# Seven block products for all but two gate/up pairs of each FFN, with their weight sums made in DRAM

## The chip, the cores and the metric

The kernel runs on one core of a Trainium2 chip. The metric is the device time of one launch in microseconds (us); the runs shown are three launches, and one more launch was taken by the profiler.

## The reference

One step of a two-layer decoder over 544 token columns (512 of a new sequence, 8 groups of 4 running ones). Each layer is FFN 1, a mixer with three recurrent branches, and FFN 2. An FFN of width 2816 on a model width of 1024 is

```
h = rmsnorm(x, g)
gate, up = split(h @ w_up, 2)          # w_up is 1024 x 5632
x = x + 0.5 * ((silu(gate) * up) @ w_down)
```

All in float32.

## The kernel before

**Tiling.** Activations lie transposed: 128 rows of a feature tile by 544 token columns. A weight tile ("piece") is 128 x 1024, that is eight 128 x 128 blocks along the contraction. Every product is done in three matmul passes on split operands: a high part (rounded to the matmul's format) and a low part (the rest) of weights and of activations, as high x high, high x low and low x high. A dense tile is 8 blocks x 3 passes x 2 halves of 272 columns, 48 matmuls (`dense`, L536).

**Two gate/up tiles as one 2 x 2 problem.** A gate tile and its up tile together are a 2 x 2 block matrix (gate or up, first or second half of the contraction) times activations in 2 x 2 blocks (halves of contraction and of tokens). `fast` (L584) computes this with seven products and 15 sums (Strassen's method in Winograd's form): A11, S2, S1, A12, S3, S4, A22 are the seven weight operands, 12 matmuls of 272 columns each, 84 in place of 96. The four sums of activations are made once for each FFN (`combined`, L1301 to L1313). The four sums of weights, S1 to S4, are made for each pair by VectorE in `weights` (L1340 to L1345) from the four blocks in `pair`. Each operand then needs a high part (ScalarE, L919) and a low part (VectorE L1349 for A11, S2, S1, A12; GpSimd L507 for S3, S4, A22). The products land in the PSUM banks SA and SB, and VectorE and ScalarE combine them into gate and up (L1384 to L1402, L925, L930), Silu (L933) and the hidden tile, whose high and low part are made at L935 and L1333.

**Staging.** An FFN has 22 hidden tiles in three blocks of 8, 8 and 6. Per block: its gate/up tiles, then eight down tiles that add to x. Before, the gate/up tiles come in turns of two dense tiles (one hidden tile) and one pair by block products (the next hidden tile), except for the first two hidden tiles of an FFN, which are four dense tiles at its start. So 10 of 22 hidden tiles go by block products (`FAST`).

**Queues.** SP issues the loads of all weights in order: dense pieces into a ring of two (`raw`), pairs into `pair`, a single buffer that is loaded again when the low parts of the pair before are made (L432). GpSimd splits each dense piece into `Wh` and `Wl` (L482, L484; a ring of two for TensorE), and between them its three low parts of a pair. GpSimd waits for `w_used`, which TensorE raises. All orders are written out; semaphores count.

## Time and profile before

| | us |
|---|---|
| runs, median (lowest to highest) | 3029.39 (3028.39 to 3030.26) |
| profiled execution, its own time | 3033.17 |
| its span, first to last instruction | 3031.4 |

The busy shares of the engines and the chain of waits are read first. The span begins at the first instruction; a row of a timeline gives the start, the busy time, the engine, line and operation, output and inputs, and in brackets how long the engine stood idle before it and which instruction ended that. The mean granted clock of TensorE over the span is 0.989 of full speed.

### The profile page before, as it was taken

The page shows a single profiled execution, that of the slowest core. Times are in us where ns is not written, and L with a number is a line of the kernel's source. Part 1 is how long each engine was busy: PE and PEld are TensorE (multiplying, and loading weights), DVE is VectorE, ACT ScalarE, POOL GpSimd, SP SyncE. Part 2 cuts the span into 40 slices and gives each one's busy share as a digit, 9 for nine tenths or more (in the row PEclk, how much of TensorE's full clock was granted, in tenths as well). Part 3 has the DMA queues.
Part 4 walks back from the last instruction along what each step waited for, and adds up shares of the span by engine and source line. Part 5 has one row for each costly group of instructions (what it writes and reads, how often), then busy time and mean ns, then how long its engine had stood idle before and what let it go on. Part 6 is the DMA issues. An engine that isn't in the chain of part 4 may idle for free.

```text
span 3031.4 us, 65367 instructions
## 1 busy us (share of the span) xinstructions
PE 2964.1 (98%) x23664; PEld 2876.5 (95%) x23664; DVE 1602.5 (53%) x2155; ACT 786.5 (26%) x1296; POOL 1752.3 (58%) x1604
## 2 busy tenths in 40 slices
PE   7999999999999999999999999999999999999998
PEld 7999999989988999999999999999898889999998
DVE  7563665535323467364674736745353245673646
ACT  4221232031232324131241312321303323331212
POOL 5666575545543575656666665654545445766665
PEclk9999999999999999999999999999999999999999
DMA  3232232232221332222232221322312123322231
GB/s 135 79 111 87 70 127 77 67 106 68 82 70 60 106 118 100 88 86 101 74 105 84 90 98 65 125 71 66 114 63 86 63 75 112 108 89 101 80 108 68
DMA packets 115174, 271.22 MB, mean 89 GB/s; under 512 B 9240, under 2 KB 53152, under 8 KB 114720
## 3 DMA queue, kind: packets, MB, share of 16 engines
q1 hardware_dynamic: 65088, 231.76, 22.7%
q10 hardware_dynamic: 49888, 36.71, 4.0%
q8 instruction: 138, 2.26, 0.3%
q14 instruction: 60, 0.49, 0.1%
HBM read 249.92 MB, written 18.52 MB: 89 GB/s over the span
## 4 chain that ended last, share of the span: by engine, by line
PE 88%; DVE 6%; issue 2%; ACT 2%; POOL 1%; ACTq 0%; DMA 0%; PEld 0%; DVEq 0%; POOLq 0%
PE dense L536 64%; PE SA L584 8%; PE SB L584 6%; PE SA L712 1%; PE SA L797 1%; PE SA L698 1%; PE SA L641 1%; PE SA L781 1%; PE SB L793 1%; DVE tmp L1241 1%; DVE Hl L1246 1%; POOL Wl L484 0%; PE SA L683 0%; PE SA L784 0%; PE SA L630 0%
## 5 line engine op out<-in xcount | busy, mean ns | idle before, releaser
L482 POOL TENSOR_SCALAR Wh<-raw 128x512 fp32r<-128x512 f32 x740 | 542.5, 733 | 1037.2 <-PEq L541 935.5
L484 POOL TENSOR_TENSOR Wl<-raw,Wh 128x512 fp32r<-128x512 f32 x740 | 1021.2, 1380 | 61.7
L536 PE MATMUL dense<-Hh,Wh 128*128 128x272 f32 x3104 | 663.0, 295 | 23.6 <-DVE Hl L1232 10.1
L536 PE MATMUL dense<-Hh,Wl 128*128 128x272 f32 x3104 | 648.4, 291 | 0.0
L536 PE MATMUL dense<-Hl,Wh 128*128 128x272 f32 x3104 | 647.9, 290 | 0.0
L536 PEld LDWEIGHTS dense<-Hh,Wh 128*128 128x128 f32 x3104 | 493.7, 191 | 34.8 <-issue 17.6
L536 PEld LDWEIGHTS dense<-Hl,Wh 128*128 128x128 f32 x3104 | 494.9, 191 | 0.0
L536 PEld LDWEIGHTS dense<-Hh,Wl 128*128 128x128 f32 x3104 | 492.9, 192 | 0.0
L536 PE MATMUL dense<-Ah,Wh 128*128 128x272 f32 x1408 | 290.9, 288 | 4.7 <-DVE Al L1333 4.7
L536 PE MATMUL dense<-Ah,Wl 128*128 128x272 f32 x1408 | 289.5, 288 | 0.0
L536 PE MATMUL dense<-Al,Wh 128*128 128x272 f32 x1408 | 289.2, 287 | 0.0
L536 PEld LDWEIGHTS dense<-Ah,Wh 128*128 128x128 f32 x1408 | 219.2, 188 | 5.5 <-DVE Al L1333 5.5
L536 PEld LDWEIGHTS dense<-Al,Wh 128*128 128x128 f32 x1408 | 220.1, 188 | 0.0
L536 PEld LDWEIGHTS dense<-Ah,Wl 128*128 128x128 f32 x1408 | 219.3, 188 | 0.0
L507 POOL TENSOR_TENSOR Sl<-pair,Sh 128x512 fp32r<-128x512 f32 x80 | 123.1, 1539 | 162.7 <-ACT Sh L919 162.7
L1414 DVE SCALAR_TENSOR_TENSOR X<-dense,X 128x544 f32 x64 | 46.4, 725 | 298.5 <-PE dense L536 297.4
L536 PE MATMUL dense<-Mh,Wh 128*128 128x272 f32 x896 | 187.0, 290 | 7.2 <-DVE tmp L1328 5.2
L536 PE MATMUL dense<-Mh,Wl 128*128 128x272 f32 x896 | 185.7, 290 | 0.0
L536 PE MATMUL dense<-Ml,Wh 128*128 128x272 f32 x896 | 185.3, 289 | 0.0
L919 ACT ACTIVATE Sh<-pair 128x512 fp32r<-128x512 f32 x160 | 95.1, 617 | 347.7 <-DMA pair<-wst 347.7
L536 PEld LDWEIGHTS dense<-Mh,Wh 128*128 128x128 f32 x896 | 140.9, 189 | 8.3 <-issue 8.0
L536 PEld LDWEIGHTS dense<-Ml,Wh 128*128 128x128 f32 x896 | 141.1, 189 | 0.0
(423 smaller groups left out, 5246.9 us busy)
## 6 DMA issues: line engine op xcount, KB each, us to landing
raw<-wst SPq DMA_DIRECT2D x336, 512.0 KB, 3.3
pair<-wst SPq DMA_DIRECT2D x80, 512.0 KB, 4.0
raw<-wst SPq DMA_DIRECT2D x32, 384.0 KB, 2.9
x_keep<-X ACTq DMA_DIRECT2D x2, 2176.0 KB, 8.3
X<-x_keep ACTq DMA_DIRECT2D x16, 272.0 KB, 3.1
sst<-st_h ACTq DMA_DIRECT2D x8, 512.0 KB, 4.5
s_h<-sst ACTq DMA_DIRECT2D x8, 512.0 KB, 3.4
sst<-st_c ACTq DMA_DIRECT2D x8, 512.0 KB, 4.0
```

The lines of the kernel that those rows point to most:

```text
L482: pool.tensor_scalar(Wh[:, j, cs], raw[:, j, cs], 1.0, 0.0, ALU.mult, ALU.add).then_inc(glink, 1)
L484: pool.tensor_tensor(Wl[:, j, cs], raw[:, j, cs], f32(Wh[:, j, cs]), ALU.subtract).then_inc(glink, 1)
L507: pool.tensor_tensor(Sl[:, q, :], src, f32(Sh[:, q, :]), ALU.subtract).then_inc(q_lo_pool, 1)
L536: mm = pe.matmul(dps[slot][:, a, 0:HALF], w[:, ring, w0:w0 + 128], x[:, k, a * HALF:(a + 1) * HALF], start=(k == 0 and n == 0), stop=(k == ...
L584: mm = pe.matmul(out, w[:, q, k * 128:(k + 1) * 128], xs[:, k, :], start=(opens and k == 0 and m == 0), stop=(k == 3 and m == 2), skip_gro ...
L641: return pe.transpose(out, in_, idn)
L698: mm = pe.matmul(o[s0:e, :, o0:o0 + n * hf].rearrange("p h (n b) -> p h n b", b=hf), K[:, kt(br, hh), c * CH + s0:c * CH + e], qs[:, :, s0 ...
L712: mm = pe.matmul(SA[:, hh // 2, col:col + 64], K[:, kt(br, hh), c * CH:(c + 1) * CH], q, start=True, stop=True)
L781: pe.matmul(SA[:, 0, cs], V[:, h, cs], att[:, h, cs], start=True, stop=(c == 0))
L793: pe.matmul(SB[:, i, :], kts[i * SMP:(i + 1) * SMP, h, :], vblk[i * SMP:(i + 1) * SMP, :], start=True, stop=True)
L919: act.activation(Sh[:, q, :], src, ACT.Copy).then_inc(q_hi, 1)
L1414: STT(xs, dps[j % 2][:, :, 0:HALF], 0.5, xs, ALU.mult, ALU.add).then_inc(slot_free[j % 2], 1)
```

## The change

- 20 of 22 hidden tiles of every FFN go by block products, one pair after another; only the four dense tiles at the start of an FFN remain.
- The sums S2, S1, S3, S4 of all 80 pairs are made in DRAM, in `w_sums`, by transfers that GpSimd issues: copies, and transfers that add to their destination (`accum_op`). Per chunk of pairs there are eight transfers in six levels; a level begins with a wait on GpSimd for all transfers before it (`sums`). As such a transfer can only add, S1 to S4 have other signs where needed, and the sums of activations and the combinations of products change theirs.
- For the first FFN the chunks hold 1, 2, 3, 2, 6 and 6 pairs, and their levels stand between GpSimd's other work in that FFN. For each of the other three FFNs they hold 6, 8 and 6, and their levels stand after every second piece of the mixer before it: six chunks in the first layer's mixer, three in the second's.
- SP loads a pair in four transfers, 1 MB into `first` (A11, S2, S1, A12) and 0.75 MB into `second` (S3, S4, A22), the first when VectorE's low parts of the pair before are done, the second when GpSimd's are.
- VectorE makes five low parts of a pair (`DVE_LO`), GpSimd two. High and low parts of the next pair stand between the combinations of the present one, on ScalarE and VectorE.
- TensorE waits before S2, S1, S3 and A22 for single reads of PSUM instead of once before a pair.
- Loops over pieces and pairs on SP and GpSimd are written out.

The diff, cut to its core; for SP, GpSimd, ScalarE and VectorE mainly the new lines stand here, and blank lines are left out:

```
-FAST = FF_TILES // 2 - 1
+FAST = FF_TILES - 2
-UP_AT = (2, 18, 34)
-DOWN_AT = (10, 26, 40)
-FAST_AT = (-1, 3, 7)
+DOWN_AT = (4, 12, 20)
+FAST_AT = (0, FF_BLOCK - 2, 2 * FF_BLOCK - 2, FAST)
+DVE_LO = 5
...
+SUM_DMAS = 8
...
+w_sums = nc.dram_tensor("w_sums", (4, PAIRS, P, 512), F32, kind="Internal").ap()
+def gate_piece(n):
+    f, i = divmod(n, FAST)
+    return (f // 2) * PIECES + (f % 2) * FFN2_D0 + (i + 2) // FF_BLOCK * FF_BLOCK + 2 * (i + 2)
+def piece(q):
+    return first[:, q, :] if q < S3 else second[:, q - S3, :]
+def chunks(f):
+    at = FAST * f
+    cuts = (0, 1, 3, 6, 8, 14, FAST) if f == 0 else FAST_AT
+    return [(at + a, at + b) for a, b in zip(cuts, cuts[1:])]
+CHUNKS = [c for f in range(2 * DEPTH) for c in chunks(f)]
+def sums_of(n):
+    return 16 * SUM_DMAS * (1 + [a <= n < b for a, b in CHUNKS].index(True))
...
-    sp.wait_ge(q_lo, ONE + n * 4)
+def load_pair(n):
+    sp.wait_ge(q_lo, ONE + n * DVE_LO)
...
-    sp.wait_ge(q_lo_pool, ONE + n * 3)
-    for t in range(2):
-        sp.dma_start(pair[:, 2 * t:2 * t + 2, :].rearrange("p a c -> p (a c)"),
-                     wst[source + t, :, :]).then_inc(pair_in, 16)
+    at = gate_piece(n)
+    sp.dma_start(first[:, 0:4:3, :], wst[at, :, :].rearrange("p (a c) -> p a c", a=2)).then_inc(first_in, 16)
+    sp.dma_start(first[:, S2:S1 + 1, :], w_sums[0:2, n, :, :].rearrange("s p c -> p s c")).then_inc(
+        first_in, 16)
+    sp.wait_ge(q_lo_pool, ONE + n * (7 - DVE_LO))
+    sp.dma_start(second[:, 0:2, :], w_sums[2:4, n, :, :].rearrange("s p c -> p s c")).then_inc(second_in, 16)
+    sp.dma_start(second[:, 2, :], wst[at + 1, :, 512:1024]).then_inc(second_in, 16)
...
+    n0 = (L * 2 + which) * FAST
+    def pairs(a, b):
+        for n in range(n0 + a, n0 + b):
+            if n == n0 or n in [c[0] for c in CHUNKS]:
+                sp.wait_ge(sum_done, sums_of(n))
+                sp.sem_inc(pair_began, 1)
+            load_pair(n)
+    for t in range(4):
+        load(L * STREAM + p0 + t, L * PIECES + d0 + t, t % 2)
+    if which:
+        sp.wait_ge(mix_clear, L + 1)
+        sp.sem_inc(pair_began, 1)
+    elif L == 0:
+        sp.wait_ge(ssq_ready, 1)
+        sp.sem_inc(pair_began, 1)
+    pairs(0, 2)
     for b, nf in enumerate((FF_BLOCK, FF_BLOCK, FF_LAST)):
+        for m in range(KT):
+            if m == 2:
+                pairs(FAST_AT[b] + 2, min(FAST_AT[b + 1] + 2, FAST))
+            load(L * STREAM + p0 + DOWN_AT[b] + m, L * PIECES + d0 + 24 * b + 2 * nf + m, m % 2, nf * P)
...
+def flat(ap):
+    return ap.rearrange("n p c -> (n p c)").rearrange("(a b) -> a b", b=2048)
+def sums(n0, n1, level):
+    at, count = gate_piece(n0), 2 * (n1 - n0)
+    halves_of = wst[at:at + count, :, :].rearrange("(n u) p (h c) -> u h p n c", u=2, h=2)
+    G_a, G_b, U_a, U_b = halves_of[0, 0], halves_of[0, 1], halves_of[1, 0], halves_of[1, 1]
+    W2, W1, W3, W4 = (w_sums[s, n0:n1, :, :].rearrange("n p c -> p n c") for s in range(4))
+    if sent[0]:
+        pool.wait_ge(sum_done, 16 * sent[0])
+        pool.sem_inc(sum_began, 1)
+    if level == 0:
+        pool.dma_start(W1, U_a).then_inc(sum_done, 16)
+        pool.dma_start(W3, G_a).then_inc(sum_done, 16)
+    elif level == 1:
+        pool.dma_start(W1, U_b, accum_op=ALU.add).then_inc(sum_done, 16)
+        pool.dma_start(W3, U_a, accum_op=ALU.add).then_inc(sum_done, 16)
+    elif level == 2:
+        pool.dma_start(flat(w_sums[0, n0:n1, :, :]), flat(w_sums[1, n0:n1, :, :])).then_inc(sum_done, 16)
+    elif level == 3:
+        pool.dma_start(W2, G_a, accum_op=ALU.add).then_inc(sum_done, 16)
+    elif level == 4:
+        pool.dma_start(flat(w_sums[3, n0:n1, :, :]), flat(w_sums[0, n0:n1, :, :])).then_inc(sum_done, 16)
+    else:
+        pool.dma_start(W4, G_b, accum_op=ALU.add).then_inc(sum_done, 16)
+    sent[0] += 2 if level < 2 else 1
+def lows(n):
+    for q in range(DVE_LO, 7):
+        pool.wait_ge(q_hi, n * 7 + (q + 1))
+        pool.tensor_tensor(Sl[:, q, :], piece(q), f32(Sh[:, q, :]), ALU.subtract).then_inc(q_lo_pool, 1)
+def one(p, cols=1024, parts=(0, 1)):
+    split(L * STREAM + p, (L * STREAM + p) // 2, p % 2, cols, parts)
 def ffn(p0, which):
+    f = L * 2 + which
+    n0 = f * FAST
+    if f == 0:
+        one_pair, two_pairs, three_pairs, next_two, block1, block2 = chunks(0)
+        sums(*one_pair, 0)
+        one(p0)
+        sums(*one_pair, 1)
+        one(p0 + 1)
+        for level in range(2, 6):
+            sums(*one_pair, level)
+        sums(*two_pairs, 0)
+        sums(*two_pairs, 1)
+        one(p0 + 2)
+        sums(*two_pairs, 2)
+        sums(*two_pairs, 3)
+        one(p0 + 3)
+        sums(*two_pairs, 4)
+        sums(*two_pairs, 5)
+        sums(*three_pairs, 0)
+        lows(n0)
+        sums(*three_pairs, 1)
+    else:
+        for t in range(4):
+            one(p0 + t)
+        lows(n0)
     for b, nf in enumerate((FF_BLOCK, FF_BLOCK, FF_LAST)):
+        one(p0 + DOWN_AT[b], nf * P)
+        for i in range(FAST_AT[b], FAST_AT[b + 1]):
+            if i < FAST - 1:
+                lows(n0 + i + 1)
+            if f == 0 and b == 1 and i - FAST_AT[1] < 5:
+                sums(*block2, i - FAST_AT[1] + 1)
+            if f == 0 and b == 0:
+                if i < 2:
+                    sums(*three_pairs, 2 + 2 * i)
+                    sums(*three_pairs, 3 + 2 * i)
+                elif i < 4:
+                    for level in range(3 * i - 6, 3 * i - 3):
+                        sums(*next_two, level)
+        for m in range(1, KT):
+            if f == 0 and b == 0:
+                if m < 7:
+                    sums(*block1, m - 1)
+                else:
+                    sums(*block2, 0)
+            one(p0 + DOWN_AT[b] + m, nf * P)
...
+ahead = [c for f in ((1, 2), (3,))[L] for c in chunks(f)]
+for p in range(MIX_PIECES):
+    one(MIX_P0 + p, parts=(SINGLE[p],) if p in SINGLE else (0, 1))
+    if p % 2 and p // 2 < 6 * len(ahead):
+        sums(*ahead[p // 12], p // 2 % 6)
...
-    (S2, SA[:, 1, h0], True, 0, 0, (T[0][1], T[1][1])),
-    (S1, SB[:, 0, h0], True, 0, 0, (T[0][0], T[1][0])),
+    (S2, SA[:, 1, h0], True, 0, 3, (T[0][1], T[1][1])),
+    (S1, SB[:, 0, h0], True, 0, 4, (T[0][0], T[1][0])),
-    (S3, SA[:, 1, h0], False, 0, 1, (T[0][2], T[1][2])),
+    (S3, SA[:, 1, h0], False, 0, 6, (T[0][2], T[1][2])),
-    (A22, SB[:, 1, h0], True, 0, 0, (T[0][3], T[1][3]))):
-if q < S3:
-    pe.wait_ge(q_lo, ONE + n * 4 + (q + 1))
+    (A22, SB[:, 1, h0], True, 0, 5, (T[0][3], T[1][3]))):
+if q < DVE_LO:
+    pe.wait_ge(q_lo, ONE + n * DVE_LO + (q + 1))
-    pe.wait_ge(q_lo_pool, ONE + n * 3 + (q - S3 + 1))
+    pe.wait_ge(q_lo_pool, ONE + n * (7 - DVE_LO) + (q - DVE_LO + 1))
-    pe.wait_ge(prod_read, ONE + n * 5 + read)
+    pe.wait_ge(prod_read, n * 5 + read)
...
+def high(n, q):
+    if q < S3:
+        act.wait_ge(first_in, n * 32 + 32)
+    else:
+        act.wait_ge(second_in, n * 32 + 32)
+    act.wait_ge(prod_done, n * 7 + (q + 1))
+    act.activation(Sh[:, q, :], piece(q), ACT.Copy).then_inc(q_hi, 1)
+def products(i, a, b, ahead=True):
+    n = L * (2 * FAST) + (which * FAST + a) + i
+    f = L * (2 * FF_TILES) + (which * FF_TILES + 2 + a) + i
+    j = a % 2
+    act.wait_ge(prod_read, n * 5 + 3)
+    act.wait_ge(prod_done, 7 + n * 7 + 1)
+    act.activation(tmp[:, 3, 0:HALF], SA[:, 0, 0:HALF], ACT.Copy).then_inc(prod_copy, 1)
+    if ahead:
+        high(n + 1, A11)
+        high(n + 1, S2)
+    act.wait_ge(ffn_lo, f - 1)
+    act.wait_ge(prod_done, 7 + n * 7 + 3)
+    act.activation(tmp[:, j, HALF:TOK], SB[:, 0, 0:HALF], ACT.Copy).then_inc(prod_copy, 1)
+    if ahead:
+        for q in (S1, A12, S3, S4):
+            high(n + 1, q)
+    act.wait_ge(prod_read, n * 5 + 7)
+    act.wait_ge(pair_mid, n * 3 + 2)
+    act.activation(tmp[:, 4 + j, :], tmp[:, 4 + j, :], ACT.Silu).then_inc(silu_done, 1)
+    if ahead:
+        high(n + 1, A22)
+    act.wait_ge(pair_mid, n * 3 + 3)
+    at = bass.ds(i + (2 + a - b * FF_BLOCK), 1) if type(i) is not int else slice(
+        2 + a - b * FF_BLOCK, 3 + a - b * FF_BLOCK)
+    act.activation(Ah[:, at, :], tmp[:, j:j + 1, :], ACT.Copy).then_inc(ffn_hi, 1)
...
+def low(n, q):
+    dve.wait_ge(q_hi, n * 7 + (q + 1))
+    TT(Sl[:, q, :], piece(q), f32(Sh[:, q, :]), ALU.subtract).then_inc(q_lo, 1)
+def products(i, a, b, ahead=True):
+    n = L * (2 * FAST) + (which * FAST + a) + i
+    f = L * (2 * FF_TILES) + (which * FF_TILES + 2 + a) + i
+    j = a % 2
+    U, V, G, root = tmp[:, 3, :], tmp[:, j, :], tmp[:, 4 + j, :], tmp[:, 2, :]
+    def product(k):
+        dve.wait_ge(prod_done, 7 + n * 7 + k)
+    if ahead:
+        low(n + 1, A11)
+    product(2)
+    dve.wait_ge(prod_copy, n * 2 + 1)
+    TT(U[:, h1], SA[:, 1, h0], U[:, h0], ALU.subtract).then_inc(prod_read, 1)
+    if ahead:
+        low(n + 1, S2)
+        low(n + 1, S1)
+    product(4)
+    TT(G[:, h0], SA[:, 0, h0], root[:, h0], ALU.mult).then_inc(prod_read, 1)
+    if ahead:
+        low(n + 1, A12)
+    product(5)
+    TT(V[:, h0], SA[:, 1, h0], U[:, h0], ALU.subtract).then_inc(prod_read, 1)
+    dve.wait_ge(prod_copy, n * 2 + 2)
+    dve.wait_ge(prod_read, 5 + n * 5 + 3)
+    TT(V[:, h1], V[:, h0], V[:, h1], ALU.subtract).then_inc(pair_mid, 1)
+    if ahead:
+        low(n + 1, S3)
+    product(6)
+    TT(U[:, h1], SB[:, 0, h0], U[:, h1], ALU.subtract).then_inc(prod_read, 1)
+    dve.wait_ge(prod_read, 5 + n * 5 + 4)
+    TT(G[:, h1], U[:, h1], root[:, h1], ALU.mult).then_inc(pair_mid, 1)
+    dve.wait_ge(silu_done, f + 1)
+    TT(G, G, root, ALU.mult).then_inc(ffn_gate, 1)
+    product(7)
+    dve.wait_ge(pair_mid, n * 3 + 1)
+    TT(V[:, h0], V[:, h0], SB[:, 1, h0], ALU.subtract).then_inc(prod_read, 1)
+    dve.wait_ge(prod_read, 5 + n * 5 + 5)
+    dve.wait_ge(ffn_gate, f + 1)
+    TT(V, V, G, ALU.mult).then_inc(pair_mid, 1)
+    at = bass.ds(i + (2 + a - b * FF_BLOCK), 1) if type(i) is not int else slice(
+        2 + a - b * FF_BLOCK, 3 + a - b * FF_BLOCK)
+    hidden_lo(f, j, at)
```

## Rows read from the trace of the kernel before

**Rows 1.** The page: busy time and share of each engine; the chain's share by engine.
```profile
PE 2964.1 (98%) x23664; PEld 2876.5 (95%) x23664; DVE 1602.5 (53%) x2155; ACT 786.5 (26%) x1296; POOL 1752.3 (58%) x1604
...
PE 88%; DVE 6%; issue 2%; ACT 2%; POOL 1%; ACTq 0%; DMA 0%; PEld 0%; DVEq 0%; POOLq 0%
```
**Rows 2.** The chain in order of time: start, us, what (matmuls merged).
```profile
30.43 9.06 PE dense L536 x48
...
92.28 12.00 PE dense L536 x96
114.83 59.84 PE dense L536 x480
```
**Rows 3.** One turn of the loop as a window: busy us (instructions) by engine, clock, DMA.
```profile
92.28:114.83 22.55, 22.55 (x183) 22.55 (x182) 15.51 (x22) 6.94 (x14) 13.39 (x12) 1.00 0.14 47
```
**Rows 4.** Timeline of VectorE in that turn: start, us, line, operation.
```profile
99.61 1.29 DVE L1349 TENSOR_TENSOR Sl<-wsum,Sh 128x512 fp32r<-128x512 f32 x2
100.81 1.78 DVE L1349 TENSOR_TENSOR Sl<-pair,Sh 128x512 fp32r<-128x512 f32 x1
102.52 0.71 DVE L1319 TENSOR_TENSOR tmp<-dense,tmp 128x544 f32<-128x544 f32 x1
103.95 1.63 DVE L1323 TENSOR_TENSOR tmp<-tmp 128x544 f32<-128x544 f32 x1 [0.72 <-ACT tmp L922]
107.43 0.44 DVE L1384 TENSOR_TENSOR tmp<-SA,tmp 128x272 f32<-128x272 f32 x1 [1.84 <-PE SA L584]
107.79 0.71 DVE L1328 TENSOR_TENSOR tmp<-dense,tmp 128x544 f32<-128x544 f32 x1
...
113.39 0.44 DVE L1395 TENSOR_TENSOR tmp<-SB,tmp 128x272 f32<-128x272 f32 x1 [0.59 <-PE SB L584]
113.86 0.74 DVE L1397 TENSOR_TENSOR tmp<-tmp 128x272 f32<-128x272 f32 x1
115.33 1.01 DVE L1399 TENSOR_TENSOR tmp<-tmp 128x544 f32<-128x544 f32 x1 [0.73 <-ACT tmp L933]
116.26 0.43 DVE L1402 TENSOR_TENSOR tmp<-tmp,SB 128x272 f32<-128x272 f32 x1
116.72 0.72 DVE L1405 TENSOR_TENSOR tmp<-tmp 128x544 f32<-128x544 f32 x1
118.42 0.77 DVE L1333 TENSOR_TENSOR Al<-tmp,Ah 128x544 f32 x1 [0.97 <-ACT Ah L935]
119.11 0.78 DVE L1272 COPY const<-const 32x32 f32<-32x32 f32 x4
```
**Rows 5.** Timeline of GpSimd (POOL) in the same turn.
```profile
100.27 1.78 POOL L507 TENSOR_TENSOR Sl<-pair,Sh 128x512 fp32r<-128x512 f32 x1 [4.37 <-ACT Sh L919]
...
103.71 1.30 POOL L507 TENSOR_TENSOR Sl<-pair,Sh 128x512 fp32r<-128x512 f32 x1
```
**Rows 6.** Timeline of ScalarE (ACT) in the same turn.
```profile
100.10 0.62 ACT L919 ACTIVATE Sh<-wsum 128x512 fp32r<-128x512 f32 x1
...
117.58 0.66 ACT L935 ACTIVATE Ah<-tmp 128x544 f32 x1 [2.29 <-DVE tmp L1405]
```
**Rows 7.** Transfers: SP's queue; issues with size and landing; duration of an issue in ns.
```profile
q1 hardware_dynamic: 65088, 231.76, 22.7%
...
raw<-wst SPq DMA_DIRECT2D x336, 512.0 KB, 3.3
...
x_keep<-X ACTq DMA_DIRECT2D x2, 2176.0 KB, 8.3
...
L432 SPq DMA_DIRECT2D pair<-wst x80: 332/333/992, 37.0 to 2949.4; - x80
```
**Rows 8.** Timeline of GpSimd at the start: the first half of piece 2.
```profile
18.53 1.43 POOL L482 TENSOR_SCALAR Wh<-raw 128x512 fp32r<-128x512 f32 x1 [3.52 <-PEq L541]
```
**Rows 9.** GpSimd in the mixer: one split in its dense part; what it waited for.
```profile
424.81 0.63 POOL L482 TENSOR_SCALAR Wh<-raw 128x512 fp32r<-128x512 f32 x1 [1.11 <-PEq L541]
...
POOL Wh L482 <- PEq L541: 300.0, 84, 10.2
```

More of the change, by code:

```diff
@@ L67 @@
 PIECES = FFN2_D0 + FFN_PIECES
+PAIRS = DEPTH * 2 * FAST
+SUM_DMAS = 8
 G0, G1, B2, WO = 29, 61, 85, 93
@@ L513, in _ @@
                 assert single % 2 == 0 and sorted(SINGLE) == [single, single + 1]
-                run(MIX_P0, MIX_P0 + single)
-                for p, half in sorted(SINGLE.items()):
-                    split(L * STREAM + (MIX_P0 + p), (L * STREAM + (MIX_P0 + p)) // 2, p % 2, 1024, (half,))
-                run(MIX_P0 + single + 2, FFN2_P0)
+                ahead = [c for f in ((1, 2), (3,))[L] for c in chunks(f)]
[3 more added lines that the diff above has]
+                        sums(*ahead[p // 12], p // 2 % 6)
                 ffn(FFN2_P0, 1)
@@ L590, in ffn @@
                     if b == 0:
-                        up(0, 0, (norm_lo, norm_no * KT))
-                        up(1, 0, part=0)
+                        up(0, (norm_lo, norm_no * KT))
+                        up(1, part=0)
                         rms(norm_no)
-                        up(1, 0, part=1)
-                        up(2, 0)
-                        up(3, 0)
-                    with pe.Fori(1 if b == 0 else 0, nf // 2) as i:
-                        for j in range(2):
-                            up(UP_AT[b] + j, i)
-                        fast(L * (2 * FAST) + (which * FAST + FAST_AT[b]) + i)
+                        up(1, part=1)
+                        up(2)
+                        up(3)
+                    with pe.Fori(FAST_AT[b], FAST_AT[b + 1]) as i:
+                        fast(L * (2 * FAST) + which * FAST + i)
                     hidden = L * (2 * FF_TILES) + (which * FF_TILES + b * FF_BLOCK)
@@ L904, in ffn @@
                                 combined_hi(3)
+                                for q in range(7):
+                                    high(L * (2 * FAST) + which * FAST, q)
                             act.wait_ge(slot_free[1], ONE + use)
@@ L936, in ffn @@
+                    with act.Fori(0, (FAST_AT[b + 1] - FAST_AT[b]) // 2 - (b == 2)) as i:
+                        for j in range(2):
+                            products(i * 2, FAST_AT[b] + j, b)
+                    if b == 2:
+                        products(0, FAST - 2, b)
+                        products(0, FAST - 1, b, False)
                     if b == 0 and which == 0:
@@ L1209, in _ @@
             dve.sem_inc(slot_free[1], ONE)
-            dve.sem_inc(prod_read, ONE)
+            dve.sem_inc(prod_read, 5)
             dve.sem_inc(q_lo, ONE)
@@ L1407, in ffn @@
+                    with dve.Fori(0, (FAST_AT[b + 1] - FAST_AT[b]) // 2 - (b == 2)) as i:
+                        for j in range(2):
+                            products(i * 2, FAST_AT[b] + j, b)
+                    if b == 2:
+                        products(0, FAST - 2, b)
+                        products(0, FAST - 1, b, False)
                     if b == 0 and which == 0:
```

134 lines of the change are left out of this document (16 added, 118 removed).

## The prediction

> **What bounds the kernel now.** I read the page's busy shares and its chain of waits first: TensorE is busy 98% of the span and is 88% of the chain [rows 1], so a matmul taken away shortens the end unless another engine or a wait takes its place. Next the chain in order of time, which gives one turn of the feed-forward loop: two dense tiles 12.00 us, then 10.55 us until the next turn, 22.55 us in all [rows 2]. Those 10.55 us are one pair by seven block products (84 matmuls; two dense tiles are 96). The window over that turn shows TensorE busy for all of it, VectorE for 15.51 of 22.55 us, GpSimd for 13.39, ScalarE for 6.94 [rows 3]. So the loop is TensorE-bound with a third of VectorE's time free, and the change roughly halves the turn. Therefore I read VectorE's, GpSimd's and ScalarE's instructions in one turn [rows 4 to 6], then what transfers take [rows 7], and last where GpSimd has time: at the start [rows 8] and in the mixer [rows 9].
>
> **Removed: matmuls.** 40 more pairs (10 in each of four FFNs) go by block products: 12.00 - 10.55 = 1.45 us each, 40 x 1.45 = -58 us. All of it is on the path. What goes with them counts nothing by itself: VectorE's four sums per pair (0.60 each) and GpSimd's splits of the two dense pieces were done beside matmuls; they only make room for what follows. Exchanged signs, loops written out on SP and GpSimd and the start value of prod_read cost nothing: the same instructions run, and both queues stand idle at the ends of a turn.
>
> **Moved: VectorE's round per pair.** Now every pair needs five low parts, eight small combinations and one hidden low part, with no dense tile between pairs. In order on VectorE: 5 low parts at 0.60 (two of them from 99.61 to 100.81); U, G and V halves that nobody waits for at once, 3 x 0.36 (107.43 to 107.79); three halves on which the next instruction depends, 0.47 + 0.47 + 0.46 (113.39 to 113.86, 116.26 to 116.72); the G half 0.44; the wait for Silu 0.73 (114.60 to 115.33, from the row that the Silu on ScalarE releases); G times root 0.64 (0.72, less the 0.08 by which the next starts early); V times G 0.72 and the 0.98 for ScalarE's copy; the hidden low part 0.69 (118.42 to 119.11) [rows 4]. Sum: 3.00 + 1.08 + 1.40 + 0.44 + 0.73 + 0.64 + 1.70 + 0.69 = 9.68 us. ScalarE's round (seven high parts of 0.62 and four others of at most 0.66: 7.0 us) fits behind it [rows 6]. 9.68 is under 10.55, by 0.9 us.
>
> GpSimd takes that. Where a subtraction of GpSimd and one of VectorE with both operands in SBUF meet, one waits for the other: VectorE's low part, 1.29 us for two in a row, took 1.78 alone beside GpSimd's, its 0.72 us form 1.63, and GpSimd's 1.30 us form took 1.78; VectorE's form with an operand in PSUM kept its 0.71 [rows 4, 5]. Per pair GpSimd does two low parts (S4, A22), 2 x 1.30. The S4 one can start when ScalarE has its high part, 0.62 + 0.11 us after the product; VectorE is by then in its G half and wins by about 0.1 us; then G times root waits about 0.35 us for GpSimd, and V times G about 0.65 us for the A22 part. 9.68 + 1.0 = 10.7 us, 0.15 over TensorE's 10.55. What is queued behind: the U half of the next pair, which TensorE's new wait (prod_read 6, before S3) needs within 6 us of that pair's start. So TensorE stops there 0.15 us a pair: 80 x 0.15 = +12 us. The other new waits on prod_read (before S2, S1 and A22) ask for reads of the pair before and are met 3 us early. If GpSimd wins the tie, the G half waits 1.1 us instead of 0.35: 11.4 us, +68 us; if nothing meets, 0. I take the first, by the 0.1 us.
>
> The Trainium skill ("SBUF — State Buffer", SBUF: two separate sides) has this as an exclusive lock for a whole instruction, held against a VectorE operation with two SBUF inputs; the 1.78 and 1.63 us agree. It adds that descriptors of transfers issued by GpSimd are written through the same port, which no row here shows; by it the sums below would be issued later than I count.
>
> **Loads.** SP fetches 1 MB of a pair once VectorE's fifth low part of the pair before is done, and 0.75 MB after GpSimd's two. 512 KB land in 3.3 us at 337 GB/s (231.76 MB in 22.7% of the span), so 1.7 us are fixed; 1 MB takes 4.9 [rows 7]. By the round above it has 5.4 us. I cost it at nothing; each 0.1 us by which 1 MB lands later than 5.4 us would be 8 us over the 80 pairs. GpSimd's and SP's turns of the queue are otherwise empty inside a block.
>
> **Added: the sums in DRAM.** Per pair eight transfers of 256 KB in six levels, and each level makes GpSimd wait until the one before has landed. The wait is in GpSimd's own queue: behind it are the splits of dense weights (4.2 us a piece: twice 0.63 and 1.30, and some waiting for the port [rows 5, 9]) and the low parts, and TensorE waits for these. The trace has no transfer from DRAM to DRAM, none that adds and none that GpSimd issues. Bounds: a level takes at least 1.7 us plus bytes at 337 GB/s (adding as fast as copying), at most twice the bytes (an add must read its destination as well as its source); x_keep's 2.2 MB in 8.3 us agrees with the first [rows 7]. Issue: between SP's 0.33 us [rows 7] and several; I take 1 us for each transfer, and copying's rate for adding, because that is the row nearest to it. Then:
>
> - Start of the first FFN. Before, GpSimd splits piece 2 at 18.5 and TensorE starts that tile at 30.43 [rows 2, 8]. Now six levels of one pair (0.8 us of bytes, 1.7 fixed, 1 issue: 3.5 each) and two of the next chunk (1 MB: 4.8 of landing, 2 of issue) stand ahead. The split of piece 1 ends at 15.4, four levels of the first chunk at 29.4, the second chunk's level 0 is issued by 31.4 and level 1 by 37.2; then split 2, so tile 2 starts at 39.5, and tile 3 behind two more levels and a split at 48: +9.8 at its end, 54.1. Pair 1's sums land at 57 and its loads at 62, and VectorE's low part of it, queued ahead of the U half of pair 0, holds that until 63.8 where TensorE wants it at 60.1: +3.7. Together +13 us.
> - Chunks of three and two pairs: GpSimd issues the three-pair chunk's levels between the low parts at 59, 66, 74, 79, 83 and 88 us (6.4 us of landing for the first two, 3.5 to 4 for the others), so it lands at 91.5, but pair 3 could be loaded at 77.8, after pair 2's low parts: +13.7. The two-pair chunk likewise: 130 against 123.3: +6.7. Together +20 us.
> - Down tiles of the first block: one level of a six-pair chunk before each tile. Two levels of 3 MB take 11.0 us, 14.2 with the tile's weights and two issues, against 6.0 of a tile: 2 x 8.2; four of 1.5 MB 8.6: 4 x 2.6. 26.8 less 4 us that the ring of two pieces covers: +23 us.
> - Mixers: nine chunks, one level after every second piece. At first GpSimd is idle only about 1 us in a 6 us tile (the 1.11 us wait at 424.81), later half of its time (300 us idle over the mixer) [rows 9]. A 3 MB level 16 us against 12 in the dense part, a 4 MB level 19 against 16, the others fit: 2 x (2 x 4 + 2 x 3) = 28 us, less 4 us of slack for each of four: +12 us.
> - Last hidden low part of a block 0.7 us later than now, in the short blocks uncovered: +4 us.
>
> Sum: -58 + 12 + 13 + 20 + 23 + 12 + 4 = +26 us. The profiled execution took 3033.2 us, 1.8 around its span of 3031.4; the runs' median is 3029.4, 3.8 below it. 3033.2 + 26 is 3059 on the profile's footing, 3055 on the median's. I forecast slower, 3055.
>
> **Rivals.**
> 1. Faster: VectorE keeps TensorE's pace (no meeting on the port, 0 instead of +12), the mixer hides every level (0), and small levels land and issue quicker than I count, so that the first FFN loses 30 us: -58 + 30 = -28, 3001 us. For it: VectorE's round alone is 9.68, and half of GpSimd's mixer is idle. Against: six serial levels before the third tile can't be free, as GpSimd has no second queue. All hidden would be 2971.
> 2. Adding transfers cost twice their bytes. Level 1 of a six-pair chunk is then 24 us: +4 at the start, +8 on the small chunks, +19 on the down tiles, +68 in the mixers (16 more a chunk in the dense part, about 6 later, after slack). 26 + 99: 3154 us. Only six- and eight-pair chunks decide it: below about 12 us a level it disappears. The Trainium skill ("Collectives: The Full Stack", The bandwidth ceiling) says that a reducing transfer reads two sources and moved 32.35 GB/s where copying moved 62.28. No transfer here shows it.
> 3. GpSimd wins the tie in every pair: +56 on the forecast, 3111.
> 4. The gains cancel to within 6 us.
>
> **Chances.** Forecast's own case (3036 to 3095) 0.34; faster 0.36, of it 0.10 under 2995; rival 2 0.10 in full and 0.08 in part; rival 3 0.06; cancelled 0.06. Forecast and faster are near each other; I keep the slower side, as it has 0.58 with its rivals. Range 2995 to 3135: 0.10 lies under it, 0.10 over it. A measurement here tells 0.2% (6 us) from nothing. Faster 0.36, within 0.06, slower 0.58.
>
> **What the profile after would show.** Matmul count down by 480. The distance between two pairs inside a block: 10.55 says that VectorE keeps pace, 10.7 the forecast, 11.4 rival 3; with it an idle of TensorE before S3, released by VectorE's U half. TensorE's start of the third tile near 39 us, not 30. Gaps before the block's down tiles of the first FFN, released by GpSimd, and few in the other three. In the mixer GpSimd waiting for its own transfers: landing of 3 MB in 11 us (forecast) or about 20 (rival 2). The prediction is wrong if FFN 2 to 4 don't each shrink by 8 to 13 us, or if the first FFN loses less than 30 us against the time that its matmuls save.

## The result, and the profile after

The changed kernel takes 3269.6 us (median of 4 runs, 3267.3 to 3275.5) against 3028.9 us (median of 4) for the kernel before: ratio 1.08, 95% interval 1.0781 to 1.0819, slower. The forecast was 3055 us with a range that ended at 3135. The sign was right; the size was not: +241 us where +26 stood.

The page of the kernel after, whose span is 3265.4 us: the lines that answer to [rows 1] and [rows 7] (busy us, share, instructions; clock and DMA in forty slices; packets, MB and share of the queues; the chain by engine; issues with their landing):

```profile
PE 2965.7 (91%) x23184; PEld 2865.6 (88%) x23184; DVE 1646.6 (50%) x2475; ACT 975.0 (30%) x1656; POOL 1554.1 (48%) x1444
PEclk8778899899998989999999999999999999999999
DMA  6677733888778753253433443388861213334432
q0 software_dynamic: 53952, 167.78, 22.1%
PE 53%; DMA 19%; DVE 11%; issue 6%; ACT 3%; POOL 3%; PEld 3%; DVEq 1%; ACTq 0%; SPq 0%; POOLq 0%; PEldq 0%
raw<-wst SPq DMA_DIRECT2D x256, 512.0 KB, 3.6
w_sums<-wst POOLq DMA_DIRECT2D x48, 1536.0 KB, 13.4
w_sums<-wst POOLq DMA_DIRECT2D x18, 2048.0 KB, 16.7
w_sums<-w_sums POOLq DMA_DIRECT2D x16, 1536.0 KB, 6.8
```

TensorE does 480 matmuls fewer (23184 for 23664) and is busy for as long as before, 2966 us: the granted clock is below full speed in the first slices. Its share fell from 98% to 91%, and DMA, which had 0% of the chain, now has 19%. The DMA engines are busy at 60 to 80% in most of the first fourteen slices (a slice is a fortieth of the span, 82 us) and at 80% again in slices 27 to 29: the first feed-forward, the first mixer, and the dense part of the second.

Read from VectorE's last residual sum of each stage, the loss stands in three places (234 us between the profiled executions, 241 between the medians). The last four columns are experiments told of below.

| stage, us | before | after | without sums | copies, all waits | copies, no waits | half of the bytes |
|---|---|---|---|---|---|---|
| first feed-forward | 405.7 | +150.8 | +1.6 | +98.7 | +56.7 | +112.8 |
| mixer, layer 1 | 722.2 | +66.8 | +0.1 | +21.1 | +12.0 | +28.7 |
| feed-forward 2 | 388.4 | -1.3 | -1.6 | +0.2 | -1.6 | -0.1 |
| feed-forward 3 | 390.2 | +0.5 | +1.1 | +0.9 | +2.6 | -1.5 |
| mixer, layer 2 | 723.4 | +19.1 | -3.2 | +0.4 | -4.1 | -0.6 |
| feed-forward 4 | 388.4 | -2.2 | +2.6 | -2.8 | +1.1 | +1.2 |
| whole, median | 3029 | 3270 | 3031 | 3155 | 3103 | 3173 |

Two things are to be seen in it before any experiment. The sums are made during the first feed-forward and the two mixers, and these lose 237 us together. And the three other feed-forwards, with ten dense pairs replaced in each, gain 3 us together instead of 43: something there eats the saved matmuls.

The start of the first feed-forward. The chain in order of time (start us, us, what), which answers to the first line of [rows 2]:

```profile
2.13 8.27 DMA w_sums<-wst
11.54 7.98 DMA w_sums<-wst
20.08 3.37 DMA w_sums<-w_sums
24.00 5.17 DMA w_sums<-wst
29.73 2.85 DMA w_sums<-w_sums
33.12 3.90 DMA w_sums<-wst
...
89.83 14.39 DMA w_sums<-wst
```

Each row is one level of a sum (the first six are the first pair's): GpSimd issues it only when the one before has landed, and splits the weights of TensorE's next tile behind it. GpSimd's timeline shows where piece 2 went, at 18.53 before [rows 8] (an entry in brackets is the idle time before, and what ended it):

```profile
46.55 1.17 POOL L541 DMA_DIRECT2D w_sums<-wst  x1 [7.47 <-DMA w_sums<-wst]
...
48.00 1.55 POOL L516 TENSOR_SCALAR Wh<-raw 128x512 fp32r<-128x512 f32 x1
```

TensorE's waits up to the end of that feed-forward (what, us in total, times, longest), and two windows (us, busy us by engine, granted clock, DMA share, GB/s):

```profile
PE SA L686 <- DVE tmp L1469: 65.8, 9, 19.9
PE dense L638 <- POOLq L520: 63.7, 9, 22.2
```
```profile
0.00:300.00 300.00, 169.58 (x1092) 165.15 (x1093) 103.13 (x168) 70.20 (x114) 110.04 (x112) 0.77 0.71 192
300.00:557.30 257.30, 239.14 (x1850) 237.57 (x1850) 150.43 (x237) 88.28 (x162) 105.24 (x96) 0.97 0.51 152
```

GpSimd's late splits (63.7 us, POOLq is its queue) and late operands of pairs (65.8, seen as VectorE's U half that stands behind a low part whose weights aren't there) are 130 us. The rest is clock: 1092 matmuls in 300 us took 169.6 us, 0.155 us each, where a matmul at full clock takes 0.125 (12.00 / 96, [rows 2]): 33 us. Together that is 163 us, and the stage has lost 165 (the 150.8 and the 14.5 that its ten new pairs save). TensorE idles, its granted clock falls from 2.4 to 1.2 GHz for stretches (it is 0.50 from 33 to 56 us; TensorE had stood idle since 28.8 and went on doing so until 51.0), and the matmuls after each gap cost more.

A steady pair after, on VectorE, and GpSimd's two low parts in it:

```profile
1411.81 0.69 DVE L1453 TENSOR_TENSOR Sl<-first,Sh 128x512 fp32r<-128x512 f32 x1
...
1417.98 1.01 DVE L1489 TENSOR_TENSOR tmp<-tmp 128x544 f32<-128x544 f32 x1 [0.73 <-ACT tmp L1013]
...
1419.38 1.35 DVE L1495 TENSOR_TENSOR tmp<-tmp 128x544 f32<-128x544 f32 x1
1421.70 0.73 DVE L1449 TENSOR_TENSOR Al<-tmp,Ah 128x544 f32 x1 [0.97 <-ACT Ah L1019]
1422.37 0.69 DVE L1453 TENSOR_TENSOR Sl<-first,Sh 128x512 fp32r<-128x512 f32 x1
```
```profile
1417.00 3.15 POOL L557 TENSOR_TENSOR Sl<-second,Sh 128x512 fp32r<-128x512 f32 x2 [7.41 <-ACT Sh L992]
```

From 1411.81 to 1422.37 is 10.56 us, with G times root at 1.01 and V times G at 1.35 beside GpSimd's two low parts. VectorE has only the two waits in brackets left: it runs at TensorE's pace and no more.

The mixers. TensorE's waits in the first, then in the second:

```profile
PE dense L638 <- POOLq L520: 23.5, 5, 10.5
PE SA L730 <- DMA sst<-st_c: 20.9, 3, 10.3
PE SB L890 <- issue: 12.2, 1, 12.2
```
```profile
PE dense L638 <- POOLq L520: 22.5, 4, 10.8
```

In the first mixer these are GpSimd's late splits, three late loads of recurrent states (`sst`), and one idle time of 12.2 us for which the profile shows no releaser; none of the three is among the longest waits of the kernel before. In the second, the late splits alone.

### The profile page after: what moved, and what is told of

Same layout as the page of the kernel before. It is cut to its first block, busy times and chain, and to the rows that moved or that the text cites. A ratio compares the mean times of both kernels' runs of the same rounds, so it can differ in the third digit from the quotient of the medians.

```text
span 3265.4 us, 62704 instructions
## 1 busy us (share of the span) xinstructions
PE 2965.7 (91%) x23184; PEld 2865.6 (88%) x23184; DVE 1646.6 (50%) x2475; ACT 975.0 (30%) x1656; POOL 1554.1 (48%) x1444
## 4 chain that ended last, share of the span: by engine, by line
PE 53%; DMA 19%; DVE 11%; issue 6%; ACT 3%; POOL 3%; PEld 3%; DVEq 1%; ACTq 0%; SPq 0%; POOLq 0%; PEldq 0%
PE dense L638 35%; DMA w_sums<-wst 12%; PE SA L686 6%; PE SB L686 4%; PEld dense L638 3%; DVE Sl L1453 3%; DMA first<-w_sums 2%; DVE tmp L1495 2%; POOL Wl L518 1%; DMA w_sums<-w_sums 1%; DMA sst<-st_c 1%; DMA second<-wst 1%; ACT Sh L992 1%; PE SA L812 1%; ACT tmp L1013 1%
## 5 line engine op out<-in xcount | busy, mean ns | idle before, releaser
L518 POOL TENSOR_TENSOR Wl<-raw,Wh 128x512 fp32r<-128x512 f32 x580 | 784.0, 1352 | 48.4
L516 POOL TENSOR_SCALAR Wh<-raw 128x512 fp32r<-128x512 f32 x580 | 420.8, 726 | 685.7 <-PEq L643 473.1
L638 PE MATMUL dense<-Hh,Wh 128*128 128x272 f32 x2464 | 535.0, 299 | 85.6 <-POOLq L520 72.6
L557 POOL TENSOR_TENSOR Sl<-second,Sh 128x512 fp32r<-128x512 f32 x160 | 238.2, 1494 | 628.1 <-ACT Sh L992 618.7
L638 PE MATMUL dense<-Hh,Wl 128*128 128x272 f32 x2464 | 519.0, 293 | 0.0
L638 PE MATMUL dense<-Hl,Wh 128*128 128x272 f32 x2464 | 518.9, 293 | 0.0
L1453 DVE TENSOR_TENSOR Sl<-first,Sh 128x512 fp32r<-128x512 f32 x320 | 214.7, 691 | 106.9 <-ACT Sh L992 105.6
L638 PEld LDWEIGHTS dense<-Ah,Wh 128*128 128x128 f32 x1408 | 223.1, 191 | 48.4 <-POOLq L520 37.9
L992 ACT ACTIVATE Sh<-first 128x512 fp32r<-128x512 f32 x320 | 190.6, 625 | 97.2 <-DMA first<-w_sums 76.9
L992 ACT ACTIVATE Sh<-second 128x512 fp32r<-128x512 f32 x240 | 149.1, 626 | 166.2 <-PE SA L686 74.6
L686 PE MATMUL SA<-ThM,Sh 128*128 128x272 f32 x320 | 99.7, 312 | 68.6 <-DVE tmp L1469 68.6
```

What stands on the lines that cost most here:

```text
L516: pool.tensor_scalar(Wh[:, j, cs], raw[:, j, cs], 1.0, 0.0, ALU.mult, ALU.add).then_inc(glink, 1)
L518: pool.tensor_tensor(Wl[:, j, cs], raw[:, j, cs], f32(Wh[:, j, cs]), ALU.subtract).then_inc(glink, 1)
L557: pool.tensor_tensor(Sl[:, q, :], piece(q), f32(Sh[:, q, :]), ALU.subtract).then_inc(q_lo_pool, 1)
L638: mm = pe.matmul(dps[slot][:, a, 0:HALF], w[:, ring, w0:w0 + 128], x[:, k, a * HALF:(a + 1) * HALF], start=(k == 0 and n == 0), stop=(k == ...
L686: mm = pe.matmul(out, w[:, q, k * 128:(k + 1) * 128], xs[:, k, :], start=(opens and k == 0 and m == 0), stop=(k == 3 and m == 2), skip_gro ...
L992: act.activation(Sh[:, q, :], piece(q), ACT.Copy).then_inc(q_hi, 1)
```

## The experiments

Times are medians. Where a kernel leaves part of the computation out, its expectation says which.

**No sums at all.** `sums()` returns at once, and

```
-  sp.dma_start(first[:, S2:S1 + 1, :], w_sums[0:2, n, :, :]...)
+  sp.dma_start(first[:, S2:S1 + 1, :], wst[at:at + 2, :, 0:512]...)
```

> Leaves out every sum of weight blocks: GpSimd issues no transfer and waits for none, and SyncE loads the operands S1 to S4 from plain weight blocks of the same size (so the result is not the reference's); all else is the changed kernel. My theory (the transfers of the sums cost all of the loss: in the first feed-forward through TensorE's wait for late tiles and late pairs, in the mixers through GpSimd's blocked queue and the crowded DMA engines; and the later three feed-forwards gain nothing because of late operands at the block starts): 3269.6 less 151 (first feed-forward) less 86 (mixers) is 3033, with the first feed-forward's own matmuls near its old time; 3015 to 3040, so within 0.5% of the kernel before. Rival one (the sums hide the promised gain of 58 us everywhere, and without them it comes back in full): 2970 to 2990. Rival two (the loop with all pairs is itself slow, by VectorE's round or by its loads): over 3060.

Measured: 3031.2 us, ratio 1.0012 (1.0003 to 1.0022). So the sums cost 238 us, nearly the whole loss, and all that is promised by 480 fewer matmuls is gone without them too. Little of it in the pairs: but for the first two distances of a feed-forward, 54 of their 60 distances inside blocks are 10.52 to 10.81 us, also at the starts of blocks, and all 60 together are 7 us over 10.55 each. By VectorE's last sum of each block, the second and third block of the second feed-forward are shorter by 4.9 and 4.4 us (forecast 5.8 and 4.35; the second blocks of the others by 2.4 to 4.8), and the first is longer by 8. TensorE's waits in the first block of the second feed-forward (1129 to 1275 us), the kernel before and then this one:

```profile
PE dense L536 <- DVE tmp L1328: 2.6, 1, 2.6
```
```profile
PE SA L692 <- DVE Sl L1459: 6.8, 1, 6.8
PE SA L692 <- DVE tmp L1475: 3.7, 1, 3.7
```

VectorE there, in this kernel:

```profile
1160.56 1.29 DVE L1435 TENSOR_TENSOR TlH<-tx,ThH 128x1088 fp32r<-128x1088 f32 x1 [1.18 <-ACT ThH L989]
1161.77 2.49 DVE L1459 TENSOR_TENSOR Sl<-first,Sh 128x512 fp32r<-128x512 f32 x4
...
1173.45 0.69 DVE L1459 TENSOR_TENSOR Sl<-first,Sh 128x512 fp32r<-128x512 f32 x1 [5.42 <-ACT Sh L998]
```

The low parts of the first pair stand behind the norm's combinations of activations, so TensorE waits 6.8 us; and since SyncE may load pair 2 only after the last of them, its first low part comes at 1173.45. Before, dense tiles covered both: between two fast pairs stood 12 us of work that needs neither. The starts cost 14, 12, 15 and 14 us, 55 together (each from the marks of the first block, with the 4.35 us of its saved matmuls added back). At each, some 6.5 us are that wait, 7 stand between the first pair and the second (17.7 to 17.9 us apart), and 1 to 1.4 between the second and the third (11.5 to 11.9).

**VectorE's work at that start shortened.** On top of no sums, the T operands' combinations on 8 of 272 columns for two groups of four:

```
+  h0, h1 = (slice(0, 8), slice(HALF, HALF + 8)) if k > 1 else (...)
```

> The kernel without sums (3031 us), and besides the sums and differences of activations for the block products' T operands are made by VectorE on 8 of 272 columns in two of the four groups of every feed-forward's start (the result is not the reference's). That takes about 1.2 us from each of the two groups, all ahead of the first pair's low parts. My theory (at each start of a feed-forward VectorE is behind: TensorE stands 6.8 us before the first pair, where the old order had a dense tile, and 3.7 us before the second pair's loads): 2.4 us at each of four starts, 8 to 12 us less, 3019 to 3024, with the idle time of 6.8 us down to about 4.4. Rival (the first pair waits for its loads or for ScalarE's copies, and VectorE only seems late): 3028 or more.

Measured: 3020.6 us, ratio 0.9984 (0.9973 to 0.9994) against 1.0012. TensorE's waits before the first pairs, all four together, without sums and then with this edit:

```profile
PE SA L692 <- DVE Sl L1459: 26.1, 4, 6.8
```
```profile
PE SA L692 <- DVE Sl L1460: 18.9, 4, 4.8
```

Some two microseconds less in VectorE's queue are 1.8 less of TensorE's waiting at each start (26.1 to 18.9 over four), so VectorE's queue is what holds the first pair; the expected 4.4 is 4.8. That the second pair's distance comes from its late load is read from the rows above; no run tests it.

**GpSimd's first down piece behind the low parts.** No sums, and

```
-  one(p0 + DOWN_AT[b], nf * P)            # ahead of the block's lows
+  if i == FAST_AT[b + 1] - 3: one(p0 + DOWN_AT[b], nf * P)
```

> No sums, as in the first of these kernels, and besides GpSimd's split of a block's first down piece is moved behind the low parts of the block's pairs up to the third from its end, instead of ahead of them all (the result is not the reference's, since the sums are missing). My theory (that split waits for a piece that is loaded late, and holds GpSimd's low parts of the first two pairs, so that the intervals there are 12.1 and 11.6 us instead of 10.6): 3 blocks x 4 feed-forwards x 2.6 us is 31 us less than the kernel without sums alone, 2985 to 3005. Rival (the two long intervals come from the first loads of the block queueing behind the down pieces' loads on SyncE, or from VectorE): less than 8 us of difference.

Measured: 3047.2 us, 16 slower than without the edit: a miss. (One of the four runs took 7744 us, for which nothing here shows a reason; the other three are 3046.8 to 3047.5.) In one place the theory held: TensorE's second distance in a feed-forward, 11.5 to 11.9 us without sums, is 10.5 to 10.6 with the split moved (the first distance grows in two of the four, by 1.1 and 1.5 us). But the other long interval that it was to explain (11.6 us) is not there without sums, and near each block's end the moved split, which now holds two low parts, makes a distance of 11.4 to 11.8 us (12.8 on VectorE). Over twelve blocks this costs more than it gives. How the sums make that other interval is left open.

**The first feed-forward's sums alone left out.**

> Leaves out the sums of the first feed-forward alone (30 us of waiting before the third tile, small chunks and the chunks between the down tiles); its operands S1 to S4 are loaded from plain weight blocks (so the result is not the reference's). My theory: the 151 us lost there go, the mixers keep theirs: 3105 to 3130 us. Rival (part of the loss there is TensorE's lower granted clock, which stays low in the first 300 us for another reason than idling): 3140 to 3180.

Measured: 3118.4 us: 151.2 less, with the first feed-forward at 406.2 us and its clock back. The mixers keep 58 and 26, together 84 of their 86 (each by itself moved, 67 to 58 and 19 to 26). So the first feed-forward's loss stands by itself, and its low clock goes with the idling: 0.98 over the first 300 us here, 0.77 in the changed kernel.

**Copies for adds.** `accum_op=ALU.add` removed, all else kept.

> Every adding transfer is made a plain copy of the same bytes between the same places, with the same order, waits and queue (the sums are then not sums, and the result is not the reference's). My theory (an adding transfer takes about twice a copy's time for its bytes, 13.0 against 6.7 us for 1.5 MB, and this doubles what the levels cost in the first feed-forward and in the mixers): the prediction's sum with copying's rate would hold for the parts that the levels set, so about half of the 236 us goes: 3120 to 3160 us; TensorE's third tile starts near 43 us rather than 51. Rival (the price is the serial wait and issue of each level and not adding's rate): over 3210. Rival (the bytes moved in DRAM are what slows the other transfers, whatever their kind): the mixers keep their 86 us and only the first feed-forward shrinks.

Measured: 3154.9 us, the first feed-forward +98.7 instead of +150.8, mixers +21.1 and +0.4 instead of +66.8 and +19.1. So 115 of 238 us are what adding takes over copying, and 123 are there with copying.

**Copies, and no waits between levels.** Each level has its own destination, so that nothing depends:

```
-  pool.wait_ge(sum_done, 16 * sent[0])
-  pool.dma_start(W1, U_b, accum_op=ALU.add)
+  pool.dma_start(D[0], U_b)
```

> The same 120 transfers with the same bytes, issued by GpSimd at the same places, but all plain copies, each to a place of its own that nobody reads, so that GpSimd waits for none before the next; the operands S1 to S4 come from plain weight blocks and SyncE waits for no sum (the result is not the reference's). To be read against the kernel with copies and all waits, 3154.9 us, and the one with no transfer at all, 3031.2. My theory (the loss is waiting: GpSimd standing in its queue until a level has landed, and operands that come late because six levels follow one another): with the waits gone only the issues (0.5 to 0.9 us each on GpSimd) and the traffic are left, 3040 to 3080 us. Rival (the traffic itself slows the weights' and the states' loads): over 3110.

Measured: 3102.6 us, between theory and rival. Waiting (GpSimd's for levels and SyncE's for sums) was 52 of the 123 us; 71 are traffic and issues, 55 of these in the first feed-forward. TensorE's waits in its first 300 us and the loads there:

```profile
PE SA L682 <- ACT tmp L997: 20.3, 9, 3.1
...
PE dense L634 <- POOLq L517: 8.4, 3, 4.3
```
```profile
first<-wst SPq DMA_DIRECT2D x28, 512.0 KB, 4.5
raw<-wst SPq DMA_DIRECT2D x14, 512.0 KB, 8.4
second<-wst SPq DMA_DIRECT2D x14, 256.0 KB, 8.3
```

The late splits are gone (8.4 us, with copies and waits 37.9), but a raw piece lands after 8.4 us instead of 3.3 [rows 7] and a pair's last 256 KB after 8.3: the transfers crowd out the loads. In the changed kernel's own first 300 us the same two take 7.1 and 6.2 us, and without any sum 3.3 and 4.5, so the crowding is there too, somewhat weaker. My expectation had left it out. Traffic and issues are not separated by any run.

**Half of the bytes.** All levels, waits and adds on 256 of 512 columns (rows of 1 KB instead of 2; the two flat copies go by such rows too).

> Every transfer of the sums takes half of its columns, so half of the bytes, with all levels, issues, waits and adds kept; the operands S1 to S4 come from plain weight blocks, still after the wait for the sums (the result is not the reference's). To be read against 3269.6 with all bytes and 3031.2 with no transfer. My theory (the bytes at adding's slow rate are the larger part of a level, 13 us for 1.5 MB of which about 3 are fixed): a bit more than half of the 238 us goes, 3130 to 3165 us. Rival (the fixed part of a transfer, its issue on GpSimd and the number of levels are what costs): over 3200.

Measured: 3173.5 us (ratio 1.0509, 1.0461 to 1.0556), 8 above the range. Half of the bytes is worth 96 of 238 us; if the cost were a fixed part and one that goes with the bytes, that would be 46 and 192.

**The third feed-forward's sums left out.**

> Leaves out the sums of the third feed-forward, which are made in the second half of the first layer's mixer (its operands S1 to S4 come from plain weight blocks, so the result is not the reference's). My theory (there the sums' traffic makes the state loads late, 10 to 12 us instead of 4, and TensorE waits for the states: 38 of the mixer's 67 us): 33 to 42 us faster, 3228 to 3237 us. Rival (the mixer's loss is GpSimd's waiting in the dense first part alone): 3260 or more.

Measured: 3233.8 us, 36 less, as the theory had it. By stages the first mixer is 44 us shorter and the second 6 longer. In the changed kernel's first mixer (560 to 1346 us) two of the three kinds of state loads land late; without these sums TensorE doesn't wait for any there (20.9 us in the changed kernel), the 12.2 us of L890 are gone as well, and GpSimd's late splits stay (24.6 us). The changed kernel's loads of that window; in the kernel before, the same two took 4.1 and 4.8 us:

```profile
sst<-st_c ACTq DMA_DIRECT2D x4, 512.0 KB, 10.1
sst<-st_g ACTq DMA_DIRECT2D x2, 512.0 KB, 12.4
```

**Levels further apart in the second mixer.**

```
-  if p % 2 and p // 2 < 6 * len(ahead):
+  every = (2, 5)[L]                       # in the second kernel (2, 3)[L]
+  if p % every == every - 1 and p // every < 6 * len(ahead):
```

> The 18 levels of the second layer's mixer are issued after every fifth piece instead of every second; all else is the changed kernel. My theory (in the second mixer the levels cost 19 us because GpSimd, busy in the dense part, waits for a level that hasn't landed in the two pieces' time): with 30 us from level to level no wait is left, 12 to 19 us faster, 3250 to 3258 us. Rival (the traffic of the sums slows other loads there, wherever it falls): 3265 or more.

> The 18 levels of the second layer's mixer after every third piece: between the change (every second, where GpSimd stood in the dense part: 22.5 us of TensorE's waiting) and the kernel with every fifth (4.2 us there, but one state load that landed 14.5 us too late while levels ran in the second half). My theory: both are avoided, since 54 pieces end ahead of the tight state loads: 10 to 16 us under the change, 3253 to 3260. Rival (the sums' traffic costs its 18 us wherever it stands): 3265 or more.

Measured: 3266.1 us with every fifth piece (ratio 1.079, 1.0772 to 1.0808, against 1.0781 to 1.0819: no difference, and a miss), 3255.2 with every third (1.0756, 1.0739 to 1.0772: 14 less). TensorE's waits in the second mixer, every fifth, then every third:

```profile
PE SA L732 <- DMA sst<-st_c: 14.5, 1, 14.5
...
PE dense L640 <- POOLq L520: 4.2, 2, 3.2
```
```profile
PE dense L640 <- POOLq L520: 8.7, 1, 8.7
PE SA L732 <- DMA sst<-st_h: 4.9, 2, 3.7
```

GpSimd's 22.5 us of the changed kernel become 4.2, and one state load that comes 14.5 us late takes their place. Every third piece leaves 8.7 and 4.9 us of the two. Its profiled execution was the slowest of its four runs (3266 us, mixer 13.8 us over before instead of 19.1), so the trace shows 5 of the 14 us; that there is a gain is measured, its full size is not traced.

**One transfer at a time.**

> The kernel without sums, and in both mixers one single DRAM-to-DRAM transfer after every third piece, in turn: copy and add of 1.5 MB and of 256 KB, each once from weight halves (2 KB rows) and once between flat buffers (rows of 8 KB where it adds); nobody reads what they write. It prices one transfer with nothing of its kind beside it. My theory (adding moves its bytes at half of copying's rate and has a like fixed part): 1.5 MB copy 6.5 to 8, add 12 to 14 us; 256 KB copy 3, add 4 to 5 us; issue 0.5 to 0.9 for a copy and up to 1.5 for an add. Rival (adds were slow because two ran at once and beside other loads): 1.5 MB add under 9 us.

Measured in one execution (3043.7 us), 60 transfers read one by one. Landing of a copy and then an add of 1.5 MB, and of a copy and an add of 256 KB (each from a window on that one):

```profile
w_sums<-wst POOLq DMA_DIRECT2D x1, 1536.0 KB, 8.5
...
w_sums<-wst POOLq DMA_DIRECT2D x1, 1536.0 KB, 14.0
...
w_sums<-wst POOLq DMA_DIRECT2D x1, 256.0 KB, 3.8
...
w_sums<-wst POOLq DMA_DIRECT2D x1, 256.0 KB, 5.0
```

Over all: copies of 1.5 MB 7.9 to 9.9 us, adds 12.4 to 14.6 and two of 22; of 256 KB 3.4 to 5.0 and 4.7 to 5.6. Rows of 2 KB or flat buffers make little difference (medians 8.7 and 8.9 us for the large copy). From the two sizes, copying moves 1.31 MB in 5.0 us (8.8 less 3.8, medians), 262 GB/s, and adding in 7.9 (12.9 less 5.0), 166 GB/s, with 2.8 and 3.4 us fixed; these are estimates from two sizes. The rival (under 9 us where none of its kind runs beside it) is out: two adds at once are not needed to make one slow. Other loads did run beside these, so their share in the 12.9 us isn't known. It can be large: the two adds of 21.9 and 22.5 us are those that ran beside the 2.2 MB copy `x_keep` at the start of each mixer. An issue on GpSimd takes 0.56 to 1.01 us for a copy and 0.80 to 1.43 for an add.

## Why the prediction was wrong

Two steps failed. The sum priced the transfers of the weight sums (first feed-forward and mixers) at +68 us: they cost +235. And it held no term for the starts of the feed-forwards, where the removed dense tiles had covered other work: +55. By its own terms, forecast and then shown:

| term | forecast | measured |
|---|---|---|
| 480 matmuls fewer | -58 | -58 |
| VectorE's round | +12 | about +1 |
| starts of the feed-forwards, pairs behind each other | 0 | +55 |
| first feed-forward, its sums | +56 | +149 |
| mixers | +12 | +86 |
| hidden low part last, and rest | +4 | about +1 |
| sum | +26 | +234 |

The sum of the measured column is that of the profiled executions, 3267.3 less 3033.2 us. The starts are read in the kernel without sums, the first feed-forward is 150.8 less the 1.6 of that kernel, and the last line is what remains.

1. **The sums' transfers: adding at copying's rate (the step that failed first).** The prediction took "copying's rate for adding, because that is the row nearest to it". With adds replaced by copies the loss falls by 115 us, so this choice alone is half of the miss. The mechanism stood in the text as rival 2, with 0.18, and its price was nearly right: adding was to cost 99 us more than copying (31 in the first feed-forward, 68 in the mixers), and costs 115 (by the stage marks 52 and 64). Its sign came as well: two adds issued together, 3 MB and more, land after 19.6 to 29.1 us, where 11 was forecast and about 20 by the rival. But rival 2's total of 3154 us is 116 too low, since it stands on the same sum: with copying alone the sums cost 97 us in the first feed-forward and 25 in the mixers, where 56 and 12 stood. That its mixers (+80) are near the measured +86 is in part luck. Points 2 to 4 are this other half. The Trainium skill ("Collectives: The Full Stack", The bandwidth ceiling), cited there, has reducing at half of copying's rate for collectives; the single transfers here, 166 against 262 GB/s, agree with the direction, the ratio being 0.63.
2. **Fixed time of a level.** 1.7 us was derived from SyncE's loads of 512 KB. Transfers that GpSimd issues have 2.8 to 3.4 us, another 0.5 us passes from landing to the next issue, and an add's issue takes 1.44 us where it is the first and 2.02 where it is the second (medians; 1 was taken). One pair's six levels took 36 us (1.4 to 37.6) instead of 21. Hence tile 3 at 51.0 us, not 39.5; all that stands ahead of the first block's down tiles costs 81 us instead of 33, and the down tiles of that block take 83 us instead of 38 (+45; forecast +23). The other 23 us are in the second block, where the six-pair chunk's levels stand between GpSimd's low parts: the sum had no term for it.
3. **Traffic.** The forecast let a level delay only what waits for it. With copies that nobody waits for, 71 us remain, and weight pieces land there in 8.4 instead of 3.3 us. In the changed kernel's first mixer two kinds of state loads take 10 and 12 us instead of 4 and 5; the sums that run beside them cost 36 us in all. No term of the sum had this.
4. **Clock.** 33 us in the first 300: a wait's price here was more than its length, since the granted clock fell behind it.
5. **Starts of the feed-forwards (the other step that failed: not in the sum).** The prediction asked what room VectorE has inside the loop, and not at its first turn: the removed dense tiles had covered the norm's work and the first load. This takes 55 of the 58 us; without any of the sums in DRAM the change is worth nothing. The stated test ("the prediction is wrong if FFN 2 to 4 don't each shrink by 8 to 13 us") caught it: they shrank by 1.3 and 2.2 us and grew by 0.5.
6. **VectorE's round (right).** 10.7 us forecast, 10.56 measured; the two waits for the port were forecast at 0.35 and 0.65 us and are 1.01 and 1.35 us where 0.64 and 0.72 were counted, so 0.37 and 0.63. The operations were summed 0.1 us too high, and by chance that is the whole margin: VectorE fits, with nothing left. Rival 3 (11.4 a pair) didn't happen.

Points 1 to 4 overlap within the 238 us of the sums; the experiments split them as 115 for adding, 52 for waiting with copies, 71 for traffic and issue. This split depends on the order in which things are taken away: halving the bytes alone gives 96. How much of the clock's 33 us belongs to each isn't separated.

## What to carry to other kernels

Work that is moved from an engine into DRAM-to-DRAM transfers is not free just because the queue is idle: price one transfer of each kind and size alone first, multiply by the levels that follow one another, and ask who stands behind the waiting engine and whose loads share the DMA engines. When slower tiles are taken out of a loop, look at its first turn: what they covered there (norm, first load, first split) becomes bare, once for each start. Spreading transfers over more time can move the conflict to the next tight load (every fifth piece gained nothing, every third 14 us of 241); halving the bytes gained 96. Fewer levels were not tried.
